# Conditioning weights on GpSimd's DMA queue in four buffers, a layer norm shared by two engines, and matmuls in TensorE's gap

## What is computed

```python
def second_block(x, c, w_mod, b_mod, ln_g, ln_b, ...):
    c_act = jax.nn.silu(c)
    for l in range(2):
        mod = c_act @ w_mod[l] + b_mod[l]              # [2048] @ [2048, 6144]
        shift, scale, gate = jnp.split(mod, 3, axis=-1)
        h = x * (1.0 + scale[:, None]) + shift[:, None]
        y = diff_attention(h, ...) if l == 0 else forgetting_attention(h, ...)
        x = layer_norm(DN_ALPHA * x + gate[:, None] * y, ln_g[l], ln_b[l])
    return x
# before layer 1, keys and values: mod = c_act @ kv_w_mod + kv_b_mod   [2048, 4096]
```

## Time and profile before

| | us |
|---|---|
| median of 3 runs | 2598.83 |
| lowest and highest run | 2596.96, 2603.57 |
| the profiled execution | 2601.48 |
| its span, first to last instruction | 2599.7 |

### The profile page before, as it was taken

One profiled execution on the slowest core, in us unless ns is written; L12 is line 12 of the kernel. 1 busy time (PEld: TensorE's weight loads), 2 busy tenths in 40 slices (PEclk: granted clock), 3 DMA queues, 4 the chain that ended last, 5 costly groups with the idle time before them and its releaser, 6 DMA issues.

```text
span 2599.7 us, 38429 instructions
## 1 busy us (share of the span) xinstructions
PE 2554.0 (98%) x14550; PEld 2156.5 (83%) x14550; DVE 1803.6 (69%) x2342; ACT 1154.6 (44%) x1475; POOL 0.2 (0%) x4
## 2 busy tenths in 40 slices
PE   8999999999999999999999999999999999999998
PEld 8977878778888888888888888899987778999886
DVE  6897676776667777777776666776786665545756
ACT  5454333445544544444443334333486344334642
POOL 0000000000000000000000000000000000000000
PEclk9999999999999999999999999999999999999999
DMA  6777676776768888888887777888845546675464
GB/s 212 247 236 247 210 249 216 255 255 211 251 227 271 270 276 276 270 272 278 277 276 250 251 253 258 280 275 275 257 138 189 186 159 181 185 230 178 137 215 143
DMA packets 317949, 605.74 MB, mean 233 GB/s; under 512 B 27742, under 2 KB 31844, under 8 KB 316140
## 3 DMA queue, kind: packets, MB, share of 16 engines
q1 hardware_dynamic: 301628, 571.59, 68.3%
q10 hardware_dynamic: 16176, 32.15, 3.6%
HBM read 593.03 MB, written 10.62 MB: 232 GB/s over the span
## 4 chain that ended last, share of the span: by engine, by line
PE 90%; DVE 4%; DMA 2%; ACT 2%; issue 2%; SPq 0%; ACTq 0%; DVEq 0%
PE bank L661 22%; PE bank L663 22%; PE bank L662 22%; PE bank L688 5%; PE bank L686 5%; PE bank L687 5%; DMA gemv_w<-in_w_mod 2%; PE bank L604 2%; PE bank L787 1%; DVE gemv_acc L1927 1%; DVE w_lo L1908 1%; DVE conv_out L2056 1%; ACT w_hi L1281 1%; PE bank L1120 1%; PE bank L813 0%
## 5 line engine op out<-in xcount | busy, mean ns | idle before, releaser
L1908 DVE TENSOR_TENSOR w_lo<-raw,w_hi 128x1024 fp32r<-128x1024 f32 x820 | 1001.7, 1223 | 725.9 <-ACT w_hi L1281 723.9
L1281 ACT CAST w_hi<-raw 128x1024 fp32r<-128x1024 f32 x820 | 859.3, 1049 | 1347.1 <-PE bank L663 1001.7
L661 PE MATMUL bank<-w_hi,u_hi 128*128 128x512 f32 x1216 | 491.9, 404 | 6.3 <-issue 3.8
L663 PE MATMUL bank<-w_hi,u_lo 128*128 128x512 f32 x1216 | 481.2, 396 | 0.0
L662 PE MATMUL bank<-w_lo,u_hi 128*128 128x512 f32 x1216 | 480.9, 395 | 0.0
L1927 DVE SCALAR_TENSOR_TENSOR gemv_acc<-gemv_w,small,gemv_acc 128x512 f32<-128x512 f32 x480 | 357.9, 746 | 23.2 <-DMA gemv_w<-in_w_mod 21.9
L661 PE MATMUL bank<-w_hi,s_hi 128*128 128x512 f32 x744 | 300.9, 404 | 1.3 <-DVE w_lo L1908 1.2
L663 PE MATMUL bank<-w_hi,s_lo 128*128 128x512 f32 x744 | 294.2, 395 | 0.0
L662 PE MATMUL bank<-w_lo,s_hi 128*128 128x512 f32 x744 | 294.2, 395 | 0.0
L688 PE MATMUL bank<-s_hi,w_lo 128*128 128x256 f32 x1024 | 290.1, 283 | 0.0
L687 PE MATMUL bank<-s_lo,w_hi 128*128 128x256 f32 x1024 | 289.5, 283 | 0.0
(11 more groups left out here) (362 smaller groups left out, 2882.6 us busy)
## 6 DMA issues: line engine op xcount, KB each, us to landing
gemv_w<-in_w_mod SPq DMA_DIRECT2D x384, 256.0 KB, 3.2
raw<-in_w_in SPq DMA_DIRECT2D x176, 512.0 KB, 4.5
raw<-in_a_w_in SPq DMA_DIRECT2D x128, 512.0 KB, 4.5
raw<-in_w_ffn_gate SPq DMA_DIRECT2D x88, 512.0 KB, 4.6
raw<-in_w_ffn_up SPq DMA_DIRECT2D x88, 512.0 KB, 4.4
raw<-in_w_ffn_down SPq DMA_DIRECT2D x88, 512.0 KB, 4.3
gemv_w<-in_kv_w_mod SPq DMA_DIRECT2D x128, 256.0 KB, 3.5
raw<-in_kv_w SPq DMA_DIRECT2D x64, 512.0 KB, 3.7
```

What stands on the lines that cost most here:

```text
L661: pe.matmul(o, xh, w_hi[:, s, t], start=(k == 0), stop=False)
L663: ins = pe.matmul(o, xl, w_hi[:, s, t], start=False, stop=(k == 2 * units - 1))
L1281: act.copy(w_hi[:, s], raw[:, s]).then_inc(hi_done, 1)
L1908: dve.tensor_tensor(w_lo[:, s], raw[:, s], w_hi[:, s].bitcast(F32), ALU.subtract).then_inc(lo_done, 1)
```

## The change

1. **Queue and buffers.** All gemv loads leave SyncE's program; a program for GpSimd issues them in order of chunk and tile. There are four buffers and four semaphores, and the load of tile t waits for gemv_step t - 3. GpSimd starts once TensorE has used 12 units of qkv. SyncE's program keeps the products' loads alone (its loops over spill and ffn get simpler).
2. **Room.** gemv_t goes; VectorE transposes gemv_acc into bank 7 and reduces from there. Its wait for `mod_stored` of the chunk before now stands before the transpose. Two small tiles shrink.
3. **Layer norm of layer 0.** ScalarE's table load moves ahead of the second last `w_hi` of o2 (and of o3), the root of the upper half is taken before the last one, the root of the lower half alone at the end. VectorE computes minus mean times reciprocal of the upper half (`SHIFTED`), ScalarE normalizes the upper half with it (`upper_normalized`), VectorE the lower.
4. **Matmuls in the gap.** Between o2 and the first transposes TensorE does 16 matmuls of 512 columns of s_hi by itself into bank 7; nobody reads them.

```diff
+GEMV_RING = 4
-        gemv_w = place("gemv_w", [P, 2, COLS], F32)
+        gemv_w = place("gemv_w", [P, GEMV_RING, COLS], F32)
         gemv_acc = place("gemv_acc", [P, COLS], F32)
-        gemv_t = place("gemv_t", [P, COLS], F32)
...
-            def load_gemv(pr, i, j, w, col):
...
-                    sp.wait_ge(gemv_step, i * (pr.mods * KD) + (n * KD + k - 1))
-                sp.dma_start(gemv_w[:, k % 2], w[k * P:(k + 1) * P, ds(col + m * COLS, COLS)]).then_inc(gemv_landed[k % 2], 16)
...
+        @block.gpsimd
+        def _(pool):
...
+            pool.wait_ge(w_used, products["qkv"].units - RING)
+            for n in range(MOD_CHUNKS):
+                w, col = mod_source(n)
+                for k in range(KD):
+                    if n * KD + k >= GEMV_RING:
+                        pool.wait_ge(gemv_step, n * KD + k - (GEMV_RING - 1))
+                    pool.dma_start(gemv_w[:, k % GEMV_RING], w[k * P:(k + 1) * P, col:col + COLS]).then_inc(
+                        gemv_landed[k % GEMV_RING], 16)
...
             def turn_normed(c):
-                pe.wait_ge(signal("ln_out"), HALVES * (c + 1))
+                pe.wait_ge(signal("ln_out"), c + 1)
+                pe.wait_ge(signal("x_rows"), 8 + 1 + c + 1)
...
+            for n in range(16):
+                pe.matmul(bank[MODB][:], s_hi[:, n, 0:P], s_hi[:, n // 2 * 2:n // 2 * 2 + 2], start=True, stop=True)
             turn_normed(0)
...
+                def first_root():
+                    own.link(act.activation(ln_tmp[layer][:, 0, D - 1:D], sm(E5, 1), ACT.Sqrt, bias=sm(E5, 1)))
...
+                        if layer == 0 and i == pr.bodies - 1 and j == pr.units - 1:
+                            root_ln(0)
+
+                    body(name, i, nothing, between, finish=first_root if i == pr.bodies - 1 else None)
...
+            def upper_normalized(c):
+
+                act.wait_ge(signal("x_rows"), 8 + 1)
+                part = xs[:, 0, c * COLS:(c + 1) * COLS]
+                act.activation(part, part, ACT.Identity, scale=sm(RR), bias=sm(SHIFTED)).then_inc(signal("ln_out"), 1)
...
             layer_tail("o2", "d", 0, forget_weights)
+            upper_normalized(0)
+            upper_normalized(1)
...
-                    dve.transpose(gemv_t[:], gemv_acc[:]).then_inc(gemv_cut, 1)
-                    dve.wait_ge(gemv_cut, i * (pr.mods * 2) + (2 * n + 1))
                     if not (isinstance(i, int) and i * pr.mods + n == 0):
                         dve.wait_ge(mod_stored, i * (pr.mods * 16) + 16 * n)
-                    dve.tensor_reduce(gemv_sums[:], gemv_t[:].rearrange("p (b c) -> p b c", c=SQ), AX.X, ALU.add).then_inc(
+                    dve.transpose(bank[MODB][:], gemv_acc[:]).then_inc(gemv_cut, 1)
+                    dve.wait_ge(gemv_cut, i * (pr.mods * 2) + (2 * n + 1))
+                    dve.tensor_reduce(gemv_sums[:], bank[MODB][:].rearrange("p (b c) -> p b c", c=SQ), AX.X, ALU.add).then_inc(
                         gemv_cut, 1)
...
+                    dve.scalar_tensor_tensor(out=sm(SHIFTED), in0=sm(LN_MOMENTS), scalar=-1.0, in1=sm(RR), op0=ALU.mult,
+                                             op1=ALU.mult).then_inc(signal("x_rows"), 1)
...
-                for th in range(HALVES):
-                    dve.tensor_scalar(xs[:, th, part], xs[:, th, part], sm(LN_MOMENTS + 2 * th), sm(RR + th), ALU.subtract,
-                                      ALU.mult).then_inc(signal("ln_out"), 1)
+                dve.tensor_scalar(xs[:, 1, part], xs[:, 1, part], sm(LN_MOMENTS + 2), sm(RR + 1), ALU.subtract,
+                                  ALU.mult).then_inc(signal("x_rows"), 1)
```

More of the change, by code:

```diff
@@ L347, in block_kernel @@
         x_in = (sem("x_in0"), sem("x_in1"))
-        gemv_landed = (sem("gemv_landed0"), sem("gemv_landed1"))
+        gemv_landed = [sem(f"gemv_landed{s}") for s in range(GEMV_RING)]
         gemv_cut = sem("gemv_cut")
@@ L477, in _, with wide_body @@
                 signal("ws_in"), 16)
-            def load_gemv(pr, i, j, w, col):
[L481 to L488, removed]
-                    sp.wait_ge(gemv_step, i * (pr.mods * KD) + (n * KD + k - 1))
-                sp.dma_start(gemv_w[:, k % 2], w[k * P:(k + 1) * P, ds(col + m * COLS, COLS)]).then_inc(gemv_landed[k % 2], 16)
[L493 to L514, removed]
+            def wide_body(pr, i, w, col, first=0):
                 half = pr.units // 2
@@ L518, in wide_body, with two_weights @@
                     load(pr, i, j, w, j % half, col + (j // half) * COLS)
-                    gemv_behind(j, gemv, tail)
-            def two_weights(pr, i, pair, gemv, tail):
+            def two_weights(pr, i, pair):
                 for j in range(pr.units):
                     load(pr, i, j, pair[2 * j // pr.units][0], j % (pr.units // 2), i * COLS)
[L525 to L532, removed]
@@ L534, in _ @@
-            pr, last = products["qkv"], None
+            pr = products["qkv"]
             for i in range(pr.bodies):
-                gemv = gemv_of(pr, i, w_mod_2[0], (pr.mod0 + i) * COLS)
-                wide_body(pr, i, w_in[0], i * 2 * COLS, gemv, last, 0 if i else RING)
+                wide_body(pr, i, w_in[0], i * 2 * COLS, 0 if i else RING)
                 if i == 0:
                     sp.dma_start(early[:], early_const).then_inc(signal("early_in"), 16)
-                last = tail_of(pr, gemv)
@@ L541, in _ @@
             pr = products["spill"]
[L542 to L550, removed]
+            wide_body(pr, 0, w_in[0], 3 * W1)
+            with sp.Fori(1, pr.bodies) as i:
+                wide_body(pr, i, w_in[0], i * 2 * COLS + 3 * W1 + 2 * H1)
             pr = products["branch"]
-            none = gemv_of(pr, 0, None, None)
@@ L553, in _ @@
-            two_weights(pr, 0, (w_branch_gdn, w_branch_moba), none, last)
+            two_weights(pr, 0, (w_branch_gdn, w_branch_moba))
             with sp.Fori(1, pr.bodies) as i:
-                two_weights(pr, i, (w_branch_gdn, w_branch_moba), none, None)
-            last = None
+                two_weights(pr, i, (w_branch_gdn, w_branch_moba))
             pr = products["w_out"]
             for i in range(pr.bodies):
[L560 to L563, removed]
+                wide_body(pr, i, w_out[0], i * 2 * COLS)
@@ L564, in _ @@
             pr = products["ffn"]
[L565 to L572, removed]
@@ L573, in _ @@
-            last = tail_of(pr, gemv_of(pr, pr.bodies - 1, w_mod_2[1], (pr.bodies - 1) * COLS + first))
+            two_weights(pr, 0, (w_ffn_gate, w_ffn_up))
+            with sp.Fori(1, pr.bodies) as i:
+                two_weights(pr, i, (w_ffn_gate, w_ffn_up))
             for name, w, col0 in (
@@ L580, in _ @@
                 for i in range(pr.bodies):
-                    gemv = gemv_of(pr, i, *(mod_source(pr.mod0 + i * pr.mods) if pr.mods else (None, None)))
-                    wide_body(pr, i, w, i * 2 * COLS + col0, gemv, last)
-                    last = tail_of(pr, gemv)
+                    wide_body(pr, i, w, i * 2 * COLS + col0)
             for n in range(2 * HALVES):
@@ L1781, in between @@
                             extra(i, j)
[L1784 to L1793 removed]
+                        if layer == 0 and i == pr.bodies - 1 and j == pr.units - 1:
+                            root_ln(0)
+                    body(name, i, nothing, between, finish=first_root if i == pr.bodies - 1 else None)
+                if layer:
+                    root_ln(0)
+                root_ln(1)
+            def upper_normalized(c):
+                act.wait_ge(signal("x_rows"), 8 + 1)
+                part = xs[:, 0, c * COLS:(c + 1) * COLS]
+                act.activation(part, part, ACT.Identity, scale=sm(RR), bias=sm(SHIFTED)).then_inc(signal("ln_out"), 1)
             def out_copy(p, h, width):
@@ L1867, in between @@
                 def between(j, i=i):
+                    if i == 0 and j < 2:
+                        upper_normalized(2 + j)
                     if i == 0 and j < 3:
```

43 lines of the change are left out of this document (22 added, 21 removed).

## The result

| | before | after |
|---|---|---|
| median of 19 runs, us | 2599.82 | 2604.44 |
| lowest, highest | 2596.96, 2603.57 | 2601.85, 2606.38 |
| span of the profiled execution | 2599.7 | 2604.5 |
| ratio, 95% interval | | 1.0018 (1.0012 to 1.0025) |

The kernel is 4.6 us slower, where 11.2 us less were forecast. By the bound of 0.3% (7.8 us) this is no change, but the interval lies wholly on the slower side.

What follows compares the result with a forecast made beforehand. TensorE, busy 98% of the span, was taken as the bound, losing time only to waits and low clock. Gains of 6.6 (qkv), 2.0 (spill) and 2.6 us (layer norm) made 11.2, from 2598.8 to 2587.6 us, range 2580 to 2600.

Steps and rivals of the forecast that it cites:

- qkv, 6.6 us: First product: earlier gemv loads remove most of TensorE's 7.3 us of waits and low clock; 6.6 us gained, bounds 0 and 7.3.
- Its cause: In qkv, gemv loads are late because only two buffers exist and SyncE issues them, standing 942 us before them.
- Spill, 2.0 us: Spill: two more gemv tiles there before the DMA crush save half of the 4.1 us loss; 2.0 us, bounds 0 and 4.1.
- The transpose into PSUM, 0: VectorE's 32 transposes and 32 reduces through a PSUM bank lie beside TensorE's work and cost nothing.
- Layer norm, 2.6 us: Between o2 and v3: earlier transposes and a clock kept up by sixteen matmuls gain 2.6 us, bounds 0.7 and 4.0.
- The second rival: The clock falls all the same at the layer norm, leaving that term 0.7 us: 2589.5 us; chance 0.10.
- Sum: 6.6 + 2.0 + 2.6 = 11.2 us off the whole kernel, for a median of 2587.6 us.
- The loads stay late: Rival: GpSimd's loads land so late that the qkv and spill gains go to about 0: 2596 us; chance 0.22.
- Saturation: Rival: slower GpSimd packets fill the DMA engines, TensorE waits over the units with gemv: 2616 us; chance 0.10 with other GpSimd losses.
- The chance of 0.10 for slower: Chance that the whole kernel gets slower, given to DMA saturation or another loss on GpSimd's side.

Runs made afterwards that it cites:

- a_sp_ring4: a_queue_only with the gemv loads back in SyncE's program at their old places, four buffers kept: 2558.17 us, ratio to before 0.9843.
- b_region_p128: The kernel before with the region of activations moved up by 128 bytes (distance 0), nothing else: 2566.15 us, ratio to before 0.9878.
- b_region_p64: The kernel before with the region of activations moved up by 64 bytes (distance 192), nothing else: 2566.16 us, ratio to before 0.9870.
- a_queue_only: a_region64 with the layer norm of the kernel before and without the sixteen matmuls: 2559.71 us, ratio to before 0.9849.
- a_rel_m64: The whole change with `small` at 408 columns, `SHIFTED` in a free column and the region at distance 192: 2553.02 us, 0.9830 of before.
- a_region64: The changed kernel with `small` narrowed by 32 columns and the region moved, giving distance 0: 2557.64 us, ratio to before 0.9835.
- a_no_mults: a_region64 without the sixteen matmuls ahead of the first normed transposes: 2557.49 us, ratio to before 0.9840.

## Why the prediction was wrong

**The step that failed** is one without a term. The change "Two small tiles shrink" and the working priced only what the tiles' instructions do. That the sizes of these and of the gemv tiles move every activation against the weights was not looked at. The prediction carried "In a stretch where it is fed, one unit (12 matmuls of 512 columns) takes 2.79 us" over to the new kernel unchanged. It goes by the layout: 2.81 us after, 2.73 us at distance 0. In place of 0, that term is 16.5 us by the product of interval and count. By medians it is the 4.6 us lost and what the rest gained at an equal distance, 8.5 us at 0 and 13.1 at 192: 13 to 18 us.

Point by point:
- **qkv, 6.6 us:** right. 6.6 at the 61st product matmul (228.35 to 221.72) with the slower interval already in it; at an equal one 7.4 (distance 0) and 6.0 (distance 192, 224.55 to 218.55). The upper bound was 7.3, so 7.4 lies just above it. The window 65 to 180 us shows it, PE busy 115.00 of 115 us.
- **Its cause** was half right. "Only two buffers exist and SyncE issues them": the first is all of it (a_sp_ring4), the second nothing. Against the rule that it cites, the prediction set SyncE's standing of 942 us; that standing only changed its place.
- **Spill, 2.0 us:** the mechanism held, the size hangs on the clock. In after the wait is 1.08 us instead of 2.39, and the low clock behind it (1.66 us) is gone: 3.0 us. At distance 0 it is worth 0.8 us, since in b_region_p128 the clock stays at 1.00 behind a wait of 2.45 us; at distance 192, where it falls in b_region_p64 (0.71 in 543 to 547 us), the lead goes from 6.0 to 9.7 us (501st product matmul 10.8, 1501st 9.7).
- **The transpose into PSUM, 0:** nothing speaks against it. a_queue_only has it in and loses nothing beyond 634 us. Alone it was not tried.
- **Layer norm, 2.6 us:** mis-sized in the profiled execution. From o2's last product matmul to the transposes some 34 us later it was 34.15 us before (2078.47 to 2112.62) and is 33.04 after (2081.22 to 2114.26): 1.1 us. The first steps came as described. The prediction counts from the end of the last matmul, 0.23 us behind its start: first transposes 3.85 us behind it (forecast 3.8), v3's first product 7.35 (forecast 7.3), clock 1.00. But the eight matmuls from 2099.14 to 2102.54 take 3.40 us instead of 1.87, 1.5 us. "I expect the clock to stay at its upper level" looked at the long gap only, not at the short gaps behind it. The second rival saw the clock fall for that reason, but ahead of v3 and with 0.7 us left; it fell later. It needn't fall: a_rel_m64's profiled execution gains 2.1 us without it. The other runs of after point the same way. The mean granted clock of its 19 runs is 0.997 in five, the profiled one among them (mean 2605.9 us), 0.998 in eight (2604.0) and 0.999 in six (2603.1). The end of the span, where nothing is multiplied, costs 0.0013 of it and each of the two low stretches of the profiled one 0.0007, so by this estimate the six had none. They too are slower than before.
- **Sum:** 11.2 us forecast for all that was priced, 11.7 in the profiled pair once the interval's 16.5 are taken out, 8.5 in the medians at distance 0 (2566.15 to 2557.64) and 13.1 at distance 192 (2566.16 to 2553.02). So the priced terms were about right together, in part by luck, as two of the three change by more than a microsecond with where the clock falls. The unpriced one was larger than their sum.
- **The loads stay late:** fell; no wait of VectorE on a transfer is left. **Saturation:** fell; the share from 1700 to 1830 us is 0.84, where it was 0.86, and PE busy throughout.
- The chance of 0.10 for slower was tied to DMA alone. Nothing in the list allowed for matmuls themselves getting slower.

One thing in after's span is not the change's: between 2443 and 2529 us it loses 2 us, at a granted clock of 0.83 (2473 to 2483) behind a gap of 1.89 us that before has too, at clock 1.00. a_region64's profiled execution shows such a fall there (0.91 in 2430 to 2445 us) and a_no_mults' none, so it doesn't come each time.

## What to carry to other kernels

Before an edit that changes a tile's size is priced, list which operands it moves against which, and compare TensorE's interval in a fed stretch of both traces before any wait is read: with some 12000 matmuls each ns counts 12 us. When a load is late, try more buffers and another queue apart; here the buffers did all of it. Keeping TensorE at work through one gap is worth nothing in an execution in which the clock falls behind the next gaps all the same, so such a filler is judged by many runs and not by one trace.

## What the runs showed of the hardware

- The start-to-start time of fed float32 matmuls depends on the distance of stationary and moving operand in SBUF modulo 256 bytes: for 512 columns 0.2274 us at 0, 0.2291 at 192, 0.2325 at 128, 0.2334 at 160, 0.2342 at 96; for 256 columns 0.1203, 0.1162, 0.1196, 0.1183, 0.1203. Distances 32, 64 and 224 weren't tried.
- A transfer of 256 KB issued by GpSimd takes its sequencer 0.54 us and lands after 4.2 to 4.3 us in the median, with two buffers or four. By SyncE's queue it takes 0.34 us (0.46 for kv_w_mod with four buffers) and lands after 3.3 to 3.4 us with two buffers and 4.4 with four.
- Behind gaps of the same place and length the clock falls in one execution and not in another: behind the gap of 1.9 us late in layer 1 it fell in after and a_region64 and not in before and a_no_mults; behind the transposes of the layer norm it fell in a_region64 and not in a_rel_m64.
